# Latent attention by head pairs over both query tiles, values on 256 columns, the column mask in the bias table, normalisation on GpSimd

## The reference

```
s_lat = jnp.where(col_in[:, None, :], s_lat, -jnp.inf).reshape(B, H, GRID_W, wr * GRID_W)
s_ctx = jnp.einsum('bhqd,bhcd->bhqc', q_r, k_ctx, preferred_element_type=jnp.float32) * scale
p = jax.nn.softmax(jnp.concatenate([s_lat, s_ctx], axis=-1), axis=-1).astype(v.dtype)
...
return jnp.einsum('bhqrk,bhrkd->bhqd', p_lat, v_s) + jnp.einsum('bhqc,bhcd->bhqd', p_ctx, v_ctx)
...
s = jnp.einsum('bgrqd,bgkd->bgrqk', q_blk, keys, preferred_element_type=jnp.float32) * (d ** -0.5)
p = jax.nn.softmax(s, axis=-1).astype(vals.dtype)
return jnp.einsum('bgrqk,bgkd->bgrqd', p, vals)
```

## Time and profile before

| | us |
|---|---|
| three timed runs | 2593.01, 2597.07, 2597.46 (median 2597.07) |
| profiled execution, its own time | 2593.24 |
| its span, first to last instruction | 2591.4 |
| TensorE busy in the span | 2217.0 (86%) |
| VectorE, ScalarE, GpSimd busy | 602.7, 391.4, 82.3 |
| attention of layer 0, first scores to the start of the projection | 1712.49 to 1797.98 |
| the same of layer 1 | 2207.48 to 2292.97 |

### The profile page before, as it was taken

How to read it: one execution, slowest core, us unless ns; L and a number is a source line. 1 busy time by engine, 2 the same in 40 slices (tenths; PEclk the granted TensorE clock), 3 DMA queues, 4 the chain that set the end, 5 groups by cost and what they waited for, 6 DMA issues and landing times. The chain is left out here.

```text
span 2591.4 us, 34059 instructions
## 1 busy us (share of the span) xinstructions
PE 2217.0 (86%) x14854; PEld 1531.9 (59%) x14854; DVE 602.7 (23%) x1276; ACT 391.4 (15%) x710; POOL 82.3 (3%) x112
## 2 busy tenths in 40 slices
PE   5998877888778878887788887899899979999997
PEld 2675453555235545564455534756788866578886
DVE  3434337001332200000002102344200033531002
ACT  1112001221131200000001201323200041321000
POOL 0024000000100000000000000100000000000000
PEclk8999887998989999999999988989999989899999
DMA  9459448799999999999999998210544722033450
GB/s 337 161 195 330 165 160 334 300 413 412 408 403 411 414 405 407 414 415 407 406 416 418 406 405 275 90 33 1 163 148 115 190 74 70 29 98 116 135 156 17
DMA packets 273052, 664.19 MB, mean 256 GB/s; under 512 B 20359, under 2 KB 138280, under 8 KB 239816
## 3 DMA queue, kind: packets, MB, share of 16 engines
q1 hardware_dynamic: 272904, 662.01, 67.9%
HBM read 660.94 MB, written 1.05 MB: 255 GB/s over the span
## 5 line engine op out<-in xcount | busy, mean ns | idle before, releaser
L963 PE MATMUL ps<-arena,ring 128*128 128x256 f32 x2368 | 519.7, 381 | 13.0 <-ACT arena L1846 10.1
L963 PEld LDWEIGHTS ps<-arena,ring 128*128 128x128 f32 x2368 | 451.7, 191 | 76.7 <-issue 10.9
L584 PE MATMUL ps<-arena,ring 128*128 128x256 f32 (+2 forms) x1648 | 380.5, 393 | 21.6 <-DMA ring<-in_w_ffn_in 11.9
L584 PEld LDWEIGHTS ps<-arena,ring 128*128 128x128 f32 (+2 forms) x1648 | 302.3, 188 | 104.3 <-issue 25.4
L1283 PE MATMUL ps<-ring,arena 128*32 128x256 f32 x4096 | 265.5, 406 | 91.7 <-DMA ring<-in_w_up 60.1
L1843 ACT ACTIVATE arena<-ps 128x512 f32<-128x512 f32 (+3 forms) x167 | 92.2, 552 | 1098.1 <-PE ps L584 488.2
L1283 PEld LDWEIGHTS ps<-ring,arena 128*32 128x32 f32 x4096 | 128.3, 115 | 215.7 <-DMA ring<-in_w_up 78.6
L1306 PE MATMUL ps<-ring,arena 128*32 128x512 f32 x1024 | 148.3, 703 | 79.3 <-DMA ring<-in_w_down 73.5
L1306 PEld LDWEIGHTS ps<-ring,arena 128*32 128x32 f32 x1024 | 30.8, 120 | 174.4 <-DMA ring<-in_w_down 113.5
L1026 PE MATMUL ps<-arena,ring 128*128 128x256 f32 x512 | 115.4, 388 | 9.7 <-issue 9.7
L1026 PEld LDWEIGHTS ps<-arena,ring 128*128 128x128 f32 x512 | 99.4, 195 | 25.8 <-issue 12.0
(11 more groups left out here) (304 smaller groups left out, 1837.0 us busy)
## 6 DMA issues: line engine op xcount, KB each, us to landing
ring<-in_w_gate SPq DMA_DIRECT2D x64, 2048.0 KB, 13.5
ring<-in_w_up SPq DMA_DIRECT2D x64, 2048.0 KB, 14.1
ring<-in_w_down SPq DMA_DIRECT2D x64, 2048.0 KB, 15.0
ring<-in_w_ada SPq DMA_DIRECT2D x36, 2048.0 KB, 12.5
ring<-in_w_ffn_in SPq DMA_DIRECT2D x64, 1024.0 KB, 7.8
ring<-in_w_ffn_out SPq DMA_DIRECT2D x16, 1408.0 KB, 7.1
ring<-in_w_in SPq DMA_DIRECT2D x9, 2048.0 KB, 8.2
ring<-in_w_out SPq DMA_DIRECT2D x6, 2048.0 KB, 8.9
```

The costliest lines, as they stand in the source:

```text
L584: m = mm(o, a, x, start=(k == 0 and r == 0), stop=(k == kt - 1 and last))
L963: m = mm(b, w[:, k, c:c + P], src[:, k, :], start=(k == 0), stop=(k == kt - 1))
```

## The change

The pairs of heads that share 128 partitions (2 hp and 2 hp + 1) are handled together, over both query tiles, so that four units make a group. Inside a group the units are ordered by query tile, then by head (`e`).

- Scores: for each query tile the two heads' 512-column calls stand next to each other and write different banks; then come both bias calls. Banks 0 to 4 are for scores, 5 and 6 for transposes, 7 for values.
- The mask call is gone. The mask, mirrored, is added to the bias table once per layer, by one GpSimd TENSOR_TENSOR of 41 x 64 columns; TensorE waits for `ww_ready` in place of the DMA's semaphore.
- Values: both query tiles at once (256 columns), eight calls per group, alternating between the two heads.
- `Pr` has eight buffers, `PT` two sets of two in other places (the unused half of `XC`, and `U`).
- VectorE keeps the maximum, the sign and the reciprocal; the multiplication of 512 columns goes to GpSimd. The copy to `oT` takes 128 x 256 once for a group.

```diff
+SCORE_BANKS, PROB_BANKS, OUT_BANKS = (0, 1, 2, 3, 4), (5, 6), (7,)
...
-        UNITS2 = [(kind, h, qt) for kind in ("na", "ga") for h in range(6) for qt in range(2)]
+        UNITS2 = [(kind, hp, qt, e) for kind in ("na", "ga") for hp in range(3) for qt in range(2) for e in range(2)]
...
-                pe.wait_ge(s_ww, 32 * (l + 1))
+                pe.wait_ge(ww_ready, l + 1)
...
+                def scores(j):
+
+                    for qt in range(2):
+                        both = []
+                        for e in range(2):
+                            kind, hp, _, _ = UNITS2[4 * j]
+                            name = f"sc{4 * j + 2 * qt + e}{N}"
+                            b = open_bank(pe, name, SCORE_BANKS)
+                            r = slice(64 * e, 64 * e + 64)
+                            q, k = (naq[r, hp], nak[r, hp]) if kind == "na" else (gaq[r, hp], gak[r, int((2 * hp + e) // 3 != e)])
+                            m = mm(b[:], q[:, P * qt:P * qt + P], k[:, keys], start=True, stop=(kind == "ga"))
+                            both.append((name, b, e))
+                            if kind == "ga":
+                                close_bank(m, name)
+                        if kind == "na":
+                            for name, b, e in both:
+                                at_ = 7 * (2 * hp + e) + 3 - 2 * qt
+                                close_bank(mm(b[:, xo:xo + T], tb2("flip64"), WW[:, at_:at_ + 4, :], start=False, stop=True), name)
...
+                def values(j):
+                    kind, hp, _, _ = UNITS2[4 * j]
+                    pe.wait_ge(pt_ready[X], NU * l + 4 * j + 4)
+                    b = open_bank(pe, f"ov{j}{N}", OUT_BANKS)
                     for k in range(4):
+                        for e in range(2):
+                            h = 2 * hp + e
...
+                            m = mm(b[64 * e:64 * e + 64, 0:T], v, PT[j % 2][e][:, k, :], start=(k == 0), stop=(k == 3))
...
+                scores(0)
+                for j in range(NU // 4):
+                    if 4 * j + 4 < NU:
+                        scores(j + 1)
+                    turn(4 * j)
+                    turn(4 * j + 1)
+                    if j:
+                        values(j - 1)
+                    turn(4 * j + 2)
+                    turn(4 * j + 3)
+                values(NU // 4 - 1)
...
+                for n in range(0, NU, 4):
+                    if n + 4 < NU:
+                        soft(n + 4)
+                        soft(n + 5)
+                    turned(n)
...
-                    step(v.reciprocal(s_, s_))
-                    step(ts(Pr[:, n % 3, :], Pr[:, n % 3, :], s_, None, ALU.mult), pn_ready[X])
...
+                    step(v.reciprocal(s_, s_), sums_inverted)
...
+                pool.wait_ge(s_ww, 32 * (l + 1))
+                step(nc.gpsimd.tensor_tensor(WW[:, 1:42, :], WW[:, 1:42, :], bc(tb2("neg_col"), 1, 41, 64), ALU.add), ww_ready)
+                for n in range(NU):
+                    pool.wait_ge(sums_inverted, NU * l + n + 1)
+                    step(nc.gpsimd.tensor_scalar(Pr[n % 8], Pr[n % 8], sm[:, n % 8:n % 8 + 1], None, ALU.mult), pn_ready[X])
```

108 lines of the change are left out of this document (46 added, 62 removed).

## The result

The changed kernel takes 2533.27 us in the median of four runs (2529.56 to 2534.34), the kernel before 2597.27 beside it (four runs, 2593.01 to 2599.57). The ratio is 0.9753, with a 95% interval of 0.9736 to 0.977: 64 us faster. The profiled execution of the changed kernel took 2529.56 us (span 2527.8), against 2593.24 before.

What follows compares the result with a forecast made beforehand. TensorE alone bounded the section; after the change GpSimd would, at 24 x 1.83 = 44 us. With start and end a section takes 60.3 instead of 85.5 us, saving 50.4 in two: 2542.8, stated as 2544, range 2528 to 2564.

Steps and rivals of the forecast that it cites:

- TensorE's prices: Attention section: score pair 0.86 us plus 0.19 return, value pair 0.43; 42 us at full clock where it was 74.6.
- Rival 2: Scores: half-height calls do not overlap, each pair 0.86 us more; section 69 us, time 2560, or 2580 with values; chance 0.10.
- The mask addition: GpSimd's addition of the mask to the bias table: about 7 us, finished before TensorE needs it, costing nothing.
- rival 3: VectorE's sign operations wait for GpSimd instructions: section 65 us (2552), or 83 us (2588) with whole waits; chance 0.08.
- GpSimd's price: GpSimd's 512-column normalise: 1.75 us each, 1.83 us from start to start.
- The low clock: Section start: the same 22 us at 1.2 GHz as before, so GpSimd goes on with unit 8 at 27.1 us.
- Rival 1: GpSimd at 1.1 us a unit or less, full clock within 8 us: section 52.3 to 55.4, time 2527 to 2533; chance 0.12.
- Rival 4: Clock stays at 1.2 GHz through the section because TensorE halts for GpSimd: section 89.3 us, time 2601; chance 0.04.
- The pace-setter: GpSimd, 24 x 1.83 = 44 us, is the section's longest queue, above TensorE's 42 and ScalarE's 40, without gap from unit 8.
- the signs that the prediction named: Section near 60 us, product near 1.75, GpSimd hardly idle from unit 8, TensorE waiting for it before ga transposes, among others.
- The sum: Section: 56.4 us to GpSimd's last product, 60.3 with what follows; 25.2 saved per layer, 50.4 in all, giving 2542.8.
- the forecast's own case: GpSimd sets the section's pace, clock rising between 8 and 31 us: 56.8 to 64.1 a section, 2536 to 2551; chance 0.63.

Runs made afterwards that it cites:

- e2: Changed kernel with adjacent score calls being two query tiles of one head, on the same 64 partitions; sections 64.78 and 65.25 us, total 2550.59 us.
- e12: Changed kernel with three transpose and four score banks, fourth copy on VectorE, two-operation GpSimd product, fourth reciprocal behind next group's first maximum; median 2523.11 us, ratio 0.9733.
- e4: Changed kernel with a group's eight value calls ordered head by head instead of alternating; sections 57.63 and 57.84 us, total 2540.03 us.
- e5: Changed kernel with GpSimd's product done twice, first by a column of ones; sections 91.23 and 91.22 us, total 2603.81 us.
- e7: Changed kernel with each group's fourth copy of transposed probabilities on VectorE instead of ScalarE; sections 54.51 and 53.22 us, total 2535.74 us.
- e8: Changed kernel with the fourth copy on VectorE and GpSimd's product written with two operations; sections 54.50 and 54.73 us, total 2531.55 us.
- e11: Changed kernel with second copy ahead of third exponential, fourth copy on VectorE, two-operation GpSimd product, two transpose banks; sections 54.53 and 51.39 us, total 2528.93 us.
- e3: Changed kernel with GpSimd's product written with a second operation, times 1.0; sections 54.90 and 54.86 us, total 2532.96 us.
- e1: Changed kernel with VectorE normalising again and GpSimd's products gone; sections 57.37 and 57.27 us, total 2537.28 us.
- e10: Changed kernel with three PSUM banks for transposes and four for scores, instead of two and five; sections 53.36 and 51.72 us, total 2534.73 us.

## Why the prediction was right, and where not

**TensorE's prices held.** A pair at the price of one head, 0.86 and 0.19 for the return: 1.06 measured to the bias (e2: 1.91 without the overlap). Values at 0.43 a pair of calls: 1.88 to the next line for four pairs. A ga group at 5.9: 5.84 in e12, where it has no wait. The mechanism of the change, halves of the array side by side, is shown by e2 and e4, which change only the order of the calls. Rival 2 is out; its 69 us a section was for all scores apart, and with those of the na half apart it is 65.

**The mask addition** was put at 7 us and took 5.73, 38 us before it was needed: hidden, as said.

**The sign operations** did not wait. All 48 took 153 to 156 ns, most of them beside one of GpSimd's products: rival 3 is out. By the Trainium skill, "SBUF — State Buffer", "SBUF: two separate sides", a VectorE operation with two inputs from SBUF or in a two-port mode and a GpSimd operation exclude each other. The one-column operations did not show that here; whether they run in such a mode, no run tells.

**GpSimd's price** was one term mis-sized: 1.75 and 1.83 from start to start, measured 1.56 and 1.65. Over 16 units that is 16 x 0.18 = 2.9 us a section.

**The low clock** was the other. The prediction took "the same 22 us at that level as before". Measured from the granted clock of the stretches, the first section had 6.8 us of it in two pieces, the second 9.3. So GpSimd's product of unit 8 began 22.3 us into the section, not 27.1. What is shown is that the 22 us come back when the pairs of the na half are taken apart (e2). Rival 1 gave the fuller array as the reason, and e2 fits that without proving it. Rival 4 had the clock fall because TensorE halts for others. In the changed kernel that came true for 3 us and not for a section, behind the waits of 1.47 and 1.04 us in the first group; in e5, where TensorE halts in every group, for about half of the section. In e12, where TensorE does not halt in the first group, the second piece is missing. The length of the halt alone does not decide it: with waits of 1.2 and 1.04 us there, layer 1 of e7 kept 2.4 GHz and layer 1 of the changed kernel and of e8 lost it, and layer 0 of e11 lost it behind 1.56 us. That stays open.

**The pace-setter** was the step that failed: "GpSimd ... is the longest queue of the section" and "from there it has no gap". It is the longest by its amount of work, and it has gaps: 0.44 to 1.30 us in each group. What it waited for was a loop through the two transpose banks, ScalarE's order of copies and the next scores, 6.97 us a group against 4 x 1.65 = 6.6. The prediction summed the engines' work and never followed a PSUM bank around. The miss was cheap because loop and queue differ by 0.4 us a group. That is luck: nothing in the prediction bounded the loop from above. e3 alone shows the miss, since it takes the longest queue away and the time stays. Of the signs that the prediction named, the section's length near 60 us and the product's near 1.75 were off in size, and two failed: GpSimd without idle time from unit 8 on, and TensorE waiting for it before transposes in the ga half. TensorE does wait there, but for ScalarE.

**The sum.** 60.3 forecast, 54.9 measured in the first section: 4.8 less until unit 8 (the clock, and GpSimd's start at 7.8 instead of 9.1), 1.7 less from there to the last product (27.6 for 29.3: the quicker product, less 2.9, against gaps of 1.4), 1.2 more behind it (5.1 for 3.9, TensorE's last transposes and values waiting for banks and copies in turn). That is 5.4 in the first section and 5.2 in the second, 10.5 together. The other 2.7 of the 13.2 us between the sum of 2542.8 and the profiled 2529.56 lie outside the sections. The stated 2544 is 10.7 above the median.

So the time lies in the stated range, but not where the forecast's own case put it: with GpSimd as the pace-setter the prediction had 56.8 to 64.1 us a section and 2536 to 2551. The measured 54.9, 55.1 and 2533.27 are at the upper edge of rival 1 (52.3 to 55.4, 2527 to 2533), which had a chance of 0.12. Of its two conditions the early clock held and the quick GpSimd did not; e3, which has it too, has the same sections. Nor did the work of TensorE and ScalarE set the pace, as rival 1 says. The gain itself was foreseen by TensorE's prices. That the number came so near is owed to the misses, the clock, the product and the pace-setter, all being small.

**What the parts are worth**, by undoing each: the overlap of the scores in the na half 9.9 and 10.1 a section, a good part of it through the 14 us more at the low clock (at most 7 us, at half the speed); the alternation of the values 2.7; the mask in the table 3.2 and 3.8; GpSimd's product 2.5 and 2.1. These come to 18 to 19 of 30.5 us. The rest, the overlap of the scores in the ga half, what e4 leaves of that of the values, their 256 columns and the fewer copies and hand-overs, was not tried apart, and since the parts share one bound they don't add.

## What to carry to other kernels

When several engines of a stage are near the same load, it may be that none of them sets the pace: follow one buffer around its loop, from the writer to the reader that frees it and through everything queued ahead of that reader, and compare that time with each engine's work. A pace that stays between 6.96 and 6.99 us while the work of three engines changes (e1, e3, e7) is the mark of such a loop. Here the third bank alone brought the scores' groups to 5.84 and 6.42 us, until GpSimd's products held the section back (e10). With the quick product, one reciprocal moved behind one maximum and one copy moved to VectorE, the section became another 4.3 and 2.7 us shorter (e12).

The Trainium skill, "TensorEngine Tiling (Array Packing)", "Performance Considerations", has the general form of it, that tiling speeds up TensorE but not the evacuation of PSUM, which both ScalarE and VectorE should share. Here sharing without the third bank (e7, e8) left the pace at 6.97 us; e12 has both, and what sharing adds to the bank no run takes apart.

## What was not expected of the hardware

- GpSimd's TENSOR_SCALAR on 512 columns took 1562 ns with one operation and 692 with two; on 256 columns has 960 and 558.
- With score calls on one half of the array at a time, full-height calls between them and no gap, TensorE was at 1.2 GHz until 22 us from the section's start (e2 and the kernel before); with the scores on both halves at once, until 5 to 6 us from it.
- Calls on the two halves overlap only with near neighbours. Sixteen value instructions of 256 columns take 1.88 us when the calls alternate and 2.79 in two runs of eight; two runs of four overlap fully (the scores of e2 in the ga half, 1.93 us against 1.92 when they alternate).
